# Down projection with tokens as weights: which side of the product moves

## The reference, cut to what matters

```python
    h = modulate(rms_norm(x, g_pre_ffn), shift_f, scale_f)
    hu_ext = jnp.concatenate([conv_hist, h @ w_up], axis=1)
    hc = b_conv
    for j in range(CONV_W):
        hc = hc + hu_ext[:, j:j + T] * w_conv[j]
    a, b = jnp.split(hc, 2, axis=-1)
    ffn = (jax.nn.gelu(a, approximate=True) * b) @ w_down
    x = x + gate_f * rms_norm(ffn, g_post_ffn)
```

## Time and profile before

| what | us |
|---|---|
| median of 3 runs | 1021.86 (1020.63 to 1022.05) |
| the profiled execution, its own time | 1020.41 |
| its span, first to last instruction | 1018.6 |
| TensorE busy within the span | 997.1 |
| VectorE busy | 472.8 |
| ScalarE busy | 387.3 |
| granted TensorE clock, mean over the span | 0.996 |

### The profile page before, as it was taken

How to read it: one execution, slowest core, us unless ns; L and a number is a source line. 1 busy time by engine, 2 the same in 40 slices (tenths; PEclk the granted TensorE clock), 3 DMA queues, 4 the chain that set the end, 5 groups by cost and what they waited for, 6 DMA issues and landing times.

```text
span 1018.6 us, 21045 instructions
## 1 busy us (share of the span) xinstructions
PE 997.1 (98%) x8961; PEld 969.8 (95%) x8961; DVE 472.8 (46%) x846; ACT 387.3 (38%) x633; POOL 112.5 (11%) x175
## 2 busy tenths in 40 slices
PE   7999999999999999999999999999999999999996
PEld 6899999999999999998989998999999999999996
DVE  6633324322532253325856448565565655432233
ACT  5334323442343224432113346454544445322132
POOL 1000300040005000325913000000000000000000
PEclk9999999999999999999999999999999999999998
DMA  9966476757666777439986671666666666565412
GB/s 321 328 236 207 152 255 230 249 178 248 236 229 224 254 262 248 149 99 363 371 310 204 216 282 56 221 220 221 228 219 227 220 223 198 195 209 188 124 46 85
DMA packets 218410, 222.34 MB, mean 218 GB/s; under 512 B 6429, under 2 KB 173725, under 8 KB 217533
## 3 DMA queue, kind: packets, MB, share of 16 engines
q1 hardware_dynamic: 218233, 220.85, 64.6%
q10 hardware_dynamic: 84, 0.15, 0.0%
HBM read 213.56 MB, written 96.03 MB: 304 GB/s over the span
## 4 chain that ended last, share of the span: by engine, by line
PE 85%; POOL 4%; DVE 3%; SPq 3%; DMA 2%; issue 2%; ACT 1%; DVEq 0%; POOLq 0%
PE acc L1514 73%; POOL cached L702 3%; SPq L403 2%; PE psT L1723 2%; PE psT L1736 1%; PE acc L1605 1%; PE psS L1706 1%; PE psS L1563 1%; DMA ada_first<-in_w_ada 1%; PE psT L1750 1%; POOL tha L709 1%; DVE w_lo L1010 1%; DMA sample_qkv<-smp_rows 1%; PE psT L1595 1%; PE psS L1704 1%
## 5 line engine op out<-in xcount | busy, mean ns | idle before, releaser
L1514 PE MATMUL acc<-act_hi,w_hi 128*128 128x260 f32 x1856 | 380.3, 286 | 1.7 <-DVE w_lo L1010 1.2
L1514 PE MATMUL acc<-act_hi,w_lo 128*128 128x260 f32 x1856 | 373.6, 283 | 0.0
L1514 PE MATMUL acc<-act_lo,w_hi 128*128 128x260 f32 x1856 | 373.1, 283 | 0.0
L1010 DVE TENSOR_TENSOR w_lo<-raw,w_hi 128x1024 fp32r<-128x1024 f32 (+1 forms) x148 | 185.1, 1252 | 319.2 <-ACT w_hi L728 318.8
L1514 PEld LDWEIGHTS acc<-act_hi,w_hi 128*128 128x128 f32 x1856 | 285.4, 188 | 8.4 <-issue 5.2
L1514 PEld LDWEIGHTS acc<-act_hi,w_lo 128*128 128x128 f32 x1856 | 285.8, 188 | 0.0
L1514 PEld LDWEIGHTS acc<-act_lo,w_hi 128*128 128x128 f32 x1856 | 285.5, 188 | 0.0
L728 ACT ACTIVATE w_hi<-raw 128x1024 fp32r<-128x1024 f32 (+1 forms) x148 | 154.7, 1047 | 140.5 <-PE acc L1514 131.5
L1514 PE MATMUL acc<-g_hi,w_hi 128*128 128x260 f32 x352 | 71.6, 284 | 0.0
L1514 PE MATMUL acc<-g_hi,w_lo 128*128 128x260 f32 x352 | 70.8, 282 | 0.0
L1514 PE MATMUL acc<-g_lo,w_hi 128*128 128x260 f32 x352 | 70.6, 282 | 0.0
(11 more groups left out here) (286 smaller groups left out, 984.9 us busy)
## 6 DMA issues: line engine op xcount, KB each, us to landing
out_k_sample<-in_cache_k_w SPq DMA_DIRECT2D x89, 368.0 KB
out_v_sample<-in_cache_v_w SPq DMA_DIRECT2D x89, 368.0 KB
raw<-in_w_in SPq DMA_DIRECT2D x60, 512.0 KB, 9.0
raw<-in_w_up SPq DMA_DIRECT2D x44, 512.0 KB, 5.5
ada_last<-in_w_ada SPq DMA_DIRECT2D x12, 1024.0 KB, 8.2
ada_first<-in_w_ada SPq DMA_DIRECT2D x16, 512.0 KB, 8.0
raw<-in_w_down SPq DMA_DIRECT2D x16, 512.0 KB, 4.4
out_k_sample<-in_cache_k_w SPq DMA_DIRECT2D x16, 511.0 KB
```

The lines of the kernel that those rows point to most:

```text
L1010: dve.tensor_tensor(w_lo[PLACE[n]][:, 0:cols], raw[:, n % RAW, 0:cols], w_hi[PLACE[n]][:, 0:cols].bitcast(F32), ALU.subtract).then_inc(lo_ ...
L1514: ins_ = pe.matmul(acc[b][:, half, 0:HALF], w, x[:, t, half * HALF:(half + 1) * HALF], start=first and i == 0 and j == 0, stop=last and i ...
```

## The change

The roles in the down projection are exchanged. The weights of a product are now 128 tokens of one tile of g (`g_hi` or `g_lo`), and 512 output features of `w_hi` or `w_lo` move; the sums are rows of tokens, in four PSUM banks (`bank`), one for each tile of 128 tokens, for one half h of the features at a time. A unit `("down", h, k)` is two k-tiles by 512 features, so there are 22, all of 512 KB, in `DOWN` order; each is used for four tiles of tokens, 24 products. For the second half the banks are taken after the first has been squared by ScalarE (`row_square`, with the sum of squares) and multiplied by the gate by VectorE (`row_take`). The last four units have slots of their own (`PLACE` 4 to 7), so that they are all there at once and go token tile by token tile: each tile is finished, squared, normed, added to `x_rows` and stored (`tile_out`) while the next is multiplied. The gate is turned into rows once (`gate_f`).

The 8 sample tokens are no longer columns of those products. `g_smp` holds their g in f32, with 24 columns of zeros, and plain f32 products on four quarters of the partitions (`sample_products`) use the unsplit `raw` weights, for two units at a time. SyncE's loads wait for them as well. They are folded with `fold_smp`, normed and turned within the last token tiles.

```diff
-    + [("down", m, part) for m in range(8) for part in range(3)]
+    + [("down", h, k) for h in range(2) for k in range(FT // 2)]
 )
+DOWN = [(h, k) for h in range(2) for k in range(FT // 2)]
+STREAM = len(DOWN) - 4
+LATER = [(d + 2,) for d in range(STREAM - 3)] + [(STREAM - 1, STREAM, STREAM + 1), (STREAM + 2, STREAM + 3)]
...
+    elif UNITS[n][0] == "down" and n - N["down", 0, 0] >= STREAM:
+        PLACE[n] = 4 + (n - N["down", 0, 0] - STREAM)
...
+                if u[0] == "down" and n - RAW >= N["down", 0, 0]:
+                    sp.wait_ge(part_done, 11 + (n - RAW - N["down", 0, 0]) // 2)
...
+            for d, (h, k) in enumerate(DOWN):
+                unit(("down", h, k), tiles(w_down)[:, 2 * k:2 * k + 2, 512 * h:512 * h + 512])
+                if d < 18 and d % 2:
+                    copy(2, 80 + d // 2)
+                if d in (2, 5, 8, 11):
+                    copy(2, 36 + (2, 5, 8, 11).index(d))
...
+            def row_square(i):
+                act.wait_ge(rowed, i + 1)
+                h, t = divmod(i, 4)
+                act.activation(ffn_rows[:, t, 512 * h:512 * h + 512], bank[t], ACT.Square, accum_out=row_sq[:, t, h:h + 1]).then_inc(row_squared, 1)
...
+            act.wait_ge(rows_turned, 2)
+            act.activation(gate_f[:, :], psT[:, :], ACT.Copy).then_inc(rows_out, 1)
+            for d in range(STREAM - 1):
+                if d == 10:
+                    for i in range(4):
+                        row_square(i)
+                done(act, ("down", *DOWN[d]))
+                for e in LATER[d]:
+                    split(N["down", 0, 0] + e)
...
+            def tile_out(t, n):
+                dve.wait_ge(row_squared, 5 + t)
+                row_mean(t)
+                row_take(4 + t)
+                row_inverse(n, slice(t, t + 1))
+                dve.wait_ge(row_taken, 5 + t)
+                row_done(t)
...
+            def row_products(slots_, t, hi, lo, first, last):
+                for a, (slot, k) in enumerate(slots_):
+                    for i in range(2):
+                        wh, wl = (w[slot][:, 512 * i:512 * i + 512] for w in (w_hi, w_lo))
+                        for j, (x, w) in enumerate(((hi, wh), (lo, wh), (hi, wl))):
+                            ins_ = pe.matmul(bank[t], x[:, k + i, t * P:(t + 1) * P], w, start=first and a + i + j == 0,
+                                             stop=last and (a, i, j) == (len(slots_) - 1, 1, 2))
+                return ins_
+
+            def sample_products(ds):
+                pe.wait_ge(g_smp_ready, 1)
+                for d in ds:
+                    h, k = DOWN[d]
+                    for i in range(2):
+                        q = 64 * (d % 2) + 32 * i
+                        ins_ = pe.matmul(smp_sums[h][q:q + 32, :], g_smp[:, 2 * k + i, :], raw[:, N["down", h, k] % RAW, 512 * i:512 * i + 512],
+                                         start=k < 2, stop=k >= FT // 2 - 2)
...
+                ins_.then_inc(part_done, 1)
+
+            pe.wait_ge(gained, 7)
+            for k in range(KT):
+                ins_ = pe.transpose(psT[:, k * P:(k + 1) * P], gg_f[:, k, PROMPT:MC].to_broadcast([P, P]), ident[:, :])
+            ins_.then_inc(rows_turned, 1)
+            evacuated(pe, ("up", FT - 1, 0))
+            evacuated(pe, ("up", FT - 1, 1))
+            for d, (h, k) in enumerate(DOWN[:STREAM]):
+                slot = ready(("down", h, k))
+                pe.wait_ge(g_lod, 2 * k + 2)
+                if d % 2:
+                    sample_products((d - 1, d))
+                for t in range(4):
+                    if (h, k) == (1, 0):
+                        pe.wait_ge(row_taken, t + 1)
+                    ins_ = row_products([(slot, 2 * k)], t, g_hi, g_lo, k == 0, (h, k) == (0, FT // 2 - 1))
...
+            four = [(ready(("down", h, k)), 2 * k) for h, k in DOWN[STREAM:STREAM + 2]]
+            sample_products((STREAM, STREAM + 1))
+            for t in range(4):
+                row_products(four[:2], t, g_hi, g_lo, False, False)
+                if t == 0:
+                    four += [(ready(("down", h, k)), 2 * k) for h, k in DOWN[STREAM + 2:]]
...
+                row_products(four[2:], t, g_hi, g_lo, False, True).then_inc(rowed, 1)
+                if t == 0:
+                    sample_products((STREAM + 2, STREAM + 3))
```

More of the change, by code:

```diff
@@ L287, in program @@
         accv = [a[:, :, 0:HALF] for a in acc]
+        bank = [acc[t // 2][:, t % 2, :] for t in range(4)]
+        smp_sums = [psS[:, 512 * h:512 * h + 512] for h in range(2)]
         psX, psN = psT[:, 512:1024], [psS[:, 512:1024], psT[:, 0:512]]
@@ L725, in split @@
                     act.wait_ge(unit_done, LAST[n] + 1)
+                elif UNITS[n][0] == "down":
+                    done(act, ("up", FT - 1, 1))
+                    if PLACE[n] >= 6:
+                        act.wait_ge(g_lod, FT)
+                        act.wait_ge(hu_tailed, 2 * FT)
                 if n == 2:
                     act.wait_ge(ada_done, SADA - 1)
-                act.activation(w_hi[PLACE[n]][:, 0:unit_cols(n)], raw[:, n % RAW, 0:unit_cols(n)], ACT.Copy).then_inc(hi_ready, 1)
+                act.activation(w_hi[PLACE[n]][:, :], raw[:, n % RAW, :], ACT.Copy).then_inc(hi_ready, 1)
             def free(s):
@@ L1006, in split @@
                 dve.wait_ge(hi_ready, SPLIT[n] + 1)
-                cols = unit_cols(n)
+                if n not in LAST and UNITS[n][0] == "down":
+                    done(dve, ("up", FT - 1, 1))
+                    if PLACE[n] >= 6:
+                        dve.wait_ge(g_lod, FT)
+                        dve.wait_ge(hu_tailed, 2 * FT)
                 if n in LAST:
                     dve.wait_ge(unit_done, LAST[n] + 1)
-                dve.tensor_tensor(w_lo[PLACE[n]][:, 0:cols], raw[:, n % RAW, 0:cols], w_hi[PLACE[n]][:, 0:cols].bitcast(F32), ALU.subtract).then_inc(lo_ready, 1)
+                dve.tensor_tensor(w_lo[PLACE[n]][:, :], raw[:, n % RAW, :], w_hi[PLACE[n]][:, :].bitcast(F32), ALU.subtract).then_inc(lo_ready, 1)
             def free(s):
@@ L1489, in _ @@
                 dve.tensor_tensor(g_lo[:, i, :], gm[m][:, :], g_hi[:, i, :].bitcast(F32), ALU.subtract).then_inc(g_lod, 1)
[L1491 to L1504, removed]
+            dve.wait_ge(g_hid, FT)
+            dve.wait_ge(g_lod, FT)
+            dve.tensor_tensor(g_smp[:, :, 0:NB], g_hi[:, :, TP:TC].bitcast(F32), g_lo[:, :, TP:TC].bitcast(F32), ALU.add).then_inc(g_smp_ready, 1)
@@ new lines, in _ @@
+            for d in range(STREAM - 1):
+                if d == 10:
+                    dve.wait_ge(rows_out, 9)
+                    for i in range(4):
+                        row_take(i)
+                for e in LATER[d]:
+                    split(N["down", 0, 0] + e)
+            tile_out(0, 4)
+            dve.wait_ge(folded, 13)
+            sums = psT[:, 0:KT * NB].rearrange("p (a b) -> p a b", a=KT)
+            mark(dve.tensor_copy(small[:, :, :], sums))
+            dve.tensor_tensor(mixS[:, :, :], sums, gg_f[:, :, 0:NB], ALU.mult)
@@ L1506, in _ @@
+            update_samples().then_inc(ys_upd, 1)
+            tile_out(2, 7)
+            tile_out(3, 8)
         @block.tensor
@@ L2037, in _ @@
                         late_fold(LATE - 1)
[L2039 to L2051, removed]
-                    pe.wait_ge(hu_tailed, 2 * FT)
[L2053 to L2069, removed]
+            def row_products(slots_, t, hi, lo, first, last):
[6 more added lines that the diff above has]
+                return ins_
```

141 lines of the change are left out of this document (106 added, 35 removed).

## The result

The changed kernel takes 1024.65 us (median of 6 runs, 1024.25 to 1025.82) against 1021.21 for the kernel before (6 runs beside them). The ratio is 1.0034, 95% interval 1.0024 to 1.0044: slower by 3.4 us, where 4.9 less than 1021.86 was forecast. The profiled execution has a span of 1022.6 us, 4.0 above that of before.

What follows compares the result with a forecast made beforehand. TensorE's own instruction stream was taken as the bound. Its last product would end 0.5 us later and the tail gain 5.6: 5.1 less than 1021.86, plus 0.2 for small waits, 1017.0 us; range 1014.5 to 1023.5.

Steps and rivals of the forecast that it cites:

- The products: Down projection: 528 products of 512 columns at 0.2156 us, 113.9 us, replace 1056 of 260 columns, 127.0; gain 13.1 us.
- (a): Rival: 0.0103 us is a fixed cost of each down-projection product; 0.226 spacing, 1022.4 us, no change; chance 0.13.
- (b): Rival: the moving operand is read at 0.462 ns a column beside a load; 0.237 spacing, 1028.2 us, slower; chance 0.06.
- (c): Rival: loads or splits come late because raw buffers are held for the samples; 1027 us, slower; chance 0.07.
- (d): Rival: the sample visits don't run four abreast, 37.8 us instead of 11.7; 1043 us; chance 0.03.
- (e): Rival: pace belongs to the pair of load and product, not the columns; 63.4 us for products, total 966; chance 0.01.
- The visits: Sample tokens in the down projection: eleven visits of four plain f32 calls on four column groups, 1.06 us each, 11.7 in all.
- The start: Start of the down projection: TensorE waits for the last up accumulator's evacuation, first product at 876.45, 1.57 us lost.
- What must hide: Down projection: splits, evacuations and loads stay covered by units of 5.17 us, slack 2.5 us, costed at nothing.
- Late work and tail: Last units: folds, samples' sum, turns and shape changes 3.2 us; after the last product 7.0 us instead of 12.6.

Runs made afterwards that it cites:

- x2: Changed kernel with most products' weights in token tiles 0 to 3 made 128, 96, 64 and 32 tokens wide, 512 columns still moving; 1023.58 us.
- x9: Kernel before, with down-projection weights only 64 features wide in all but the first and last product of each sum; 1020.92 us.
- x1: Changed kernel with most products in token tiles 0 to 3 moving 512, 384, 256 and 128 columns; 989.39 us.
- x10: Changed kernel with 512 of its 528 row products each made as two of 256 columns with the same weights; 1027.01 us, ratio 1.0069 to before.
- x4: Changed kernel with most products of token tile 1 reading upper halves of words as bf16, those of tile 3 plain f32; 1104.77 us.
- x5: Changed kernel, most products moving bf16 constants side by side (tile 1), one f32r column 512 times (tile 2), every second f32r word (tile 3); 1050.23 us.
- x6: Changed kernel with six of the eleven visits for the sample tokens left out; 1017.86 us, ratio 0.9966 to before.
- x8: Changed kernel with an earlier start of two token tiles, the last two visits joined, and fold calls replaced by turns; 1023.04 us, ratio 1.0019 to before.
- x3: Changed kernel with two token tiles done side by side in units 1 to 9, so successive products change PSUM bank; 1024.77 us.

## Why the prediction was wrong

**The step that failed** is "The products": the pace of 0.2156 taken from the plain f32 row of 520 steps. Of the 9.9 us between the predicted and the measured end of the last product, it carries 8.0 (528 x 0.0153). A plain f32 record takes two steps for each word of its moving side, so its row says nothing of reading at one word a step; it was near in form and far in the one thing that mattered. The row to go by was the kernel's own, and I explained its excess over 260 steps by a load that was about as long. x2 shows that the load takes no part at 512 columns, and x9 that it makes at most 1 of the 10 ns at 260. With the line from x1 the terms are: before, 1056 x (260 x 0.441 + 5.5) ns = 126.9 us; after, 528 x (512 x 0.441 + 5.5) = 122.1. The change saves 4.8 us there: 1.9 for 8 columns fewer in 520, and 2.9 for half the number of products. I had 13.1.

**Rivals.** (a), a fixed cost of 0.0103, fitted the 260 columns and falls with x1 and x10: the fixed part is 0.0055, and 0.231 is not 0.226. (b), the column dearer in proportion, was the case: 0.231 against its 0.237, and above its deciding point of 0.229. I gave it 0.06, on an argument (plain f32 keeps 0.421 a step) that x4 shows to be about another rate of reading. Its guess at a cause, the load beside it, is wrong, by x2; by x5 it is the moving side's own reading, whatever limits that. (c) did not happen: not one wait for a load or split stands in the chain. (d) did not: eight records in 0.99 us. (e) did not; 0.231 is nowhere near 0.120.

The Trainium skill's rule for start to start (TensorE: Matmul & The Clock Gate, "Wait — 56ns, not 53.3ns?"), by which 512 columns are 0.2158, and which I cited as agreeing, holds here for bf16 side by side and for f32r at stride 0 (0.216 each), and not for f32r words in a row (0.231). Another page of the Trainium skill (SBUF — State Buffer, "A bandwidth-pool intuition that's wrong (but worth ruling out)") puts the path of the moving operand at 2 bytes a step of 2.4 GHz and lane for bf16, and names no figure for moving words of 4 bytes. The runs here give f32r some 3.8 bytes a step (9.1/2.4), nearly twice the page's figure for bf16, and short of the 4 that one word a step would need.

**The visits** were mis-sized: 1.15 to 1.17 by x6 (1.20 by the beats) for 1.06, 1.0 to 1.4 us in all. The upper bound of 1.16, the measured visit "in full", was about right; the claim that a 512-column product would hide the late second product after the visit failed. The beat after a visit is 0.34 for 0.231, 0.10 late, as it was 0.10 late for 260 columns.

**The start** held to 0.01 us. g_smp was ready at 882.15, 0.55 ahead of the first visit at 882.70, where 0.1 had been forecast; x8, in which it is waited for, shows that 0.14 of this is needed, so 0.4 was to spare.

**What must hide** did. The split of each unit lies within the other slot's unit, and the last two loads came in time. Here the slower products gave still more room (5.5 us a unit), so this was a weaker test than planned.

**Late work and tail.** The folds, sum and turns took 3.0 for 3.2. The tail took 6.2 for 7.0: the four small steps lie 0.19 apart, where the 0.84 of the sum had them 0.21 apart; the first of them, the reciprocal, began as the gate product ended; and from the issue of the last store to the end of the span it is 2.4 and not 2.8.

The balance, on the profiled executions: won are 126.9 - 121.9 = 5.0 on products, 3.1 on 28 turns and 6.4 on the tail; paid are 13.1 for visits (by the late beats; by x6 12.8), 1.6 at the start and 3.0 for the late work. That is 3.2 us lost, and the 0.5 from ahead of the stage makes 3.7 of the 4.0 between the spans. The change turns 8 columns of 520, which cost 0.441 x 8 x 528 = 1.9 us as riders, into 13 us of work of their own; this and the products' small gain, 5 where 13.1 was hoped for, decide the sign.

## What to carry to other kernels

When a stream's spacing is a little above both of its candidates, vary one of them alone (columns, then weight width) before one is blamed; a row of another data type may read its operand at another rate. The f32r products of 256 to 512 columns here were bound by the reading of the moving side, so longer products win only the fixed few ns each, and the number of columns moved hardly changes. A few left-over rows were far cheaper here as riders in wide products: their own plain f32 instructions, with some 0.15 us for each change of shape, cost seven times as much.

## What the runs showed of the hardware

- f32r moving words in a row cost 0.441 ns a column with the granted clock at 1.00 (0.998 over the changed kernel), and 0.0055 a product: 0.231, 0.175 and 0.118 us for 512, 384 and 256 columns (x1). With stride 0 the same instruction takes 0.216 to 0.219, with stride 8 bytes 0.453 (x5).
- 512 bf16 moving columns take 0.216 side by side (x5) and 0.226 at stride 4 bytes (x4). Plain f32 takes 0.4285 a record of 512 (x4).
- Weight width (128 to 32 columns, x2) and a change of PSUM bank (x3) have no effect on the spacing at 512 columns. At 128 columns the spacing is 0.112 (x1), the pace of the load; by the line the load would take over below some 240 columns, (0.112 - 0.0055)/0.000441, an estimate.
- A visit of eight records with 32 weight columns each costs 1.15 to 1.17 us in a stream of 512-column products (x6): 0.86 of its own and 0.3 for the two changes of shape.
- The doubled time at stride 8 was not expected: the Trainium skill (SBUF — State Buffer, "Door 1: The DMA port swizzle (why [64,N] ≈ [32,N])") lets f32 stride up to four words for free, within lines of 16 bytes. For TensorE's moving side here two words already double the time (0.453 for 0.231).
